# Attention of three transformer layers: banks dealt out anew in the forgetting attention, and ScalarE's copies ahead of its exponentials

## What is computed

```python
s = einsum('bqhd,bkhd->bhqk', qb, k) * scale
s = s + (cb[..., :, None] - c[..., None, :])      # c: running sum of log forget gates
s = where(qpos[:, None] >= kpos[None, :], s, -inf)
p = softmax(s, axis=-1)
out = einsum('bhqk,bkhd->bqhd', p, v)
```

## Time and profile before

| | busy us | share of the span |
|---|---|---|
| TensorE matmul | 2302.1 | 92% |
| VectorE | 1358.3 | 54% |
| ScalarE | 860.4 | 35% |
| GpSimd | 781.0 | 31% |

### The profile page before, as it was taken

The page is one execution under the profiler, slowest core; times in us unless marked ns, Lnnn a source line. Parts: engine busy times, 40 slices in busy tenths (PEclk is TensorE's granted clock), DMA queues, the critical chain, the costliest instruction groups (busy, mean ns, idle before and its releaser), DMA issues. The chain is left out here.

```text
span 2493.3 us, 32515 instructions
## 1 busy us (share of the span) xinstructions
PE 2302.1 (92%) x11689; PEld 1858.5 (75%) x11689; DVE 1358.3 (54%) x2272; ACT 860.4 (35%) x1347; POOL 781.0 (31%) x370
## 2 busy tenths in 40 slices
PE   5998998899999999898868899999998799999998
PEld 4777986778788888776756788877676557888876
DVE  4587655577604771465344577721497563677601
ACT  3425212433313332324323333322323564333322
POOL 2000001334443444332101444444464003344442
PEclk8999998999999999899887999999999899999999
DMA  3320001223332333232101333333332002233232
GB/s 116 93 77 1 1 2 32 72 81 100 98 96 78 99 101 101 73 93 58 45 18 35 93 93 100 97 86 87 89 85 60 1 1 85 84 93 93 87 98 85
DMA packets 346541, 179.78 MB, mean 72 GB/s; under 512 B 16840, under 2 KB 343619, under 8 KB 346443
## 3 DMA queue, kind: packets, MB, share of 16 engines
q1 hardware_dynamic: 344842, 177.36, 24.8%
q10 hardware_dynamic: 1056, 1.06, 0.1%
q0 software_dynamic: 544, 0.06, 0.0%
HBM read 176.33 MB, written 2.13 MB: 72 GB/s over the span
## 5 line engine op out<-in xcount | busy, mean ns | idle before, releaser
L298 POOL TENSOR_TENSOR wlo<-raw,whi 128x1024 fp32r<-128x1024 f32 (+3 forms) x327 | 743.0, 2276 | 1641.6 <-ACT whi L294 994.7
L311 PE MATMUL banks<-xhi,whi 128*128 128x512 f32 x1536 | 610.6, 398 | 5.1 <-DVE cb L1036 3.9
L313 PE MATMUL banks<-xhi,wlo 128*128 128x512 f32 x1536 | 601.6, 392 | 0.0
L312 PE MATMUL banks<-xlo,whi 128*128 128x512 f32 x1536 | 601.6, 392 | 0.0
L311 PEld LDWEIGHTS banks<-xhi,whi 128*128 128x128 f32 x1536 | 291.3, 190 | 72.8 <-issue 9.1
L312 PEld LDWEIGHTS banks<-xlo,whi 128*128 128x128 f32 x1536 | 291.2, 190 | 64.0 <-issue 3.8
L313 PEld LDWEIGHTS banks<-xhi,wlo 128*128 128x128 f32 x1536 | 290.6, 189 | 60.9
L877 ACT ACTIVATE whi<-raw 128x1024 fp32r<-128x1024 f32 (+1 forms) x216 | 209.8, 981 | 194.5 <-DMA raw<-in_ffn_w_out_dram 90.4
L965 ACT ACTIVATE cb<-banks,conv 128x512 f32<-128x512 f32 x152 | 118.0, 779 | 445.5 <-DVE banks L1025 445.5
L311 PE MATMUL banks<-ghi,whi 128*128 128x512 f32 x608 | 239.3, 394 | 19.8 <-DVE xT L1067 13.8
L312 PE MATMUL banks<-glo,whi 128*128 128x512 f32 x608 | 237.8, 391 | 0.0
(11 more groups left out here) (451 smaller groups left out, 3090.7 us busy)
## 6 DMA issues: line engine op xcount, KB each, us to landing
raw<-in_ffn_w_in_dram SPq DMA_DIRECT2D x88, 512.0 KB, 3.9
raw<-in_w_ffn_up_dram SPq DMA_DIRECT2D x64, 512.0 KB, 4.1
raw<-in_w_ffn_down_dram SPq DMA_DIRECT2D x32, 512.0 KB, 4.4
raw<-in_ev_w_in_dram SPq DMA_DIRECT2D x25, 512.0 KB, 4.0
raw<-in_ffn_w_out_dram SPq DMA_DIRECT2D x32, 384.0 KB, 3.7
raw<-in_ffn_w_out_dram SPq DMA_DIRECT2D x32, 320.0 KB, 3.3
raw<-in_od_w_in_dram SPq DMA_DIRECT2D x20, 512.0 KB, 3.9
raw<-in_w_in_dram SPq DMA_DIRECT2D x19, 512.0 KB, 3.9
```

What stands on the lines that cost most here:

```text
L298: return pool.tensor_tensor(wlo[c][:, 0:n, :], raw[b][:, 0:n, :], whi[c][:, 0:n, :].bitcast(F32), ALU.subtract)
L311: pe.matmul(acc, whi[b][:, k, :], hi(k), start=first and k == 0, stop=False)
L312: pe.matmul(acc, whi[b][:, k, :], lo(k), start=False, stop=False)
L313: mm = pe.matmul(acc, wlo[b][:, k, :], hi(k), start=False, stop=last and k == n - 1)
```

## The change

Stage C: score banks (0, 1) alone, turn banks 2 and 3, output banks 4 and 5, and banks 6 and 7 in turn for spreads and fillers. The sums move to step 1, the root to ScalarE's step 2, the spreads to steps 3 and 4 (two each), and the fillers to steps 7, 9, 11, 13, 15, 17, 18 and 19; a filler now waits for the add of the filler two before it. In every stage, ScalarE's step makes the copy of i-2 first and the exponentials of i second, and in stage B ScalarE copies the turned values ahead of the attention steps of its tile.

```diff
--- before.py
+++ after.py
@@ -1200,6 +1200,15 @@
             dve.tensor_copy(self.pt[n % 4][:, 0:w], bank[self.t_banks[n % len(self.t_banks)]][:, 0:w]).then_inc(self.ptaken[1].h, 1)
 
         def act(self, act, i):
+            u = i - self.FLIP
+            if 0 <= u < self.U:
+                w = self.units[u]["w"]
+                if u >= 2:
+                    act.wait_ge(self.weighed.h, u - 1)
+                act.wait_ge(self.flipped.h, u * self.J + 1)
+                to = 2 * w if self.joined else w
+                act.activation(self.pt[u * self.J % (2 * self.J)][:, 0:to], bank[self.t_banks[u * self.J % len(self.t_banks)]][:, 0:to], ACT.Copy)\
+                    .then_inc(self.ptaken[0].h, 1)
             u = i
             if u < self.U:
                 w, e = self.units[u]["w"], self.ex[u % self.NE]
@@ -1209,15 +1218,6 @@
                 if self.sink is not None:
                     ins = act.activation(self.f(u, "sink"), self.f(u, "sink"), ACT.Exp)
                 ins.then_inc(self.exped.h, 1)
-            u = i - self.FLIP
-            if 0 <= u < self.U:
-                w = self.units[u]["w"]
-                if u >= 2:
-                    act.wait_ge(self.weighed.h, u - 1)
-                act.wait_ge(self.flipped.h, u * self.J + 1)
-                to = 2 * w if self.joined else w
-                act.activation(self.pt[u * self.J % (2 * self.J)][:, 0:to], bank[self.t_banks[u * self.J % len(self.t_banks)]][:, 0:to], ACT.Copy)\
-                    .then_inc(self.ptaken[0].h, 1)
 
     def attend(units, sink=None, lam=None):
 
@@ -1997,6 +1997,10 @@
                     for t in (2 * (m - V0 - 5), 2 * (m - V0 - 5) + 1):
                         act.wait_ge(vb_turned.h, t + 1)
                         act.activation(vtb[:, t, :, :].rearrange("p m n -> p (m n)"), bank[4 + t % 2][:, :], ACT.Copy).then_inc(vb_taken.h, 1)
+                if A0 + 6 <= m < A0 + 10:
+                    t = m - A0 - 6
+                    act.wait_ge(va_turned.h, t + 1)
+                    act.activation(vta[:, t, :, :].rearrange("p m n -> p (m n)"), bank[7][:, :], ACT.Copy).then_inc(va_taken.h, 1)
                 for half in range(2):
                     if step(m, half) >= 0:
                         at.act(act, step(m, half))
@@ -2005,10 +2009,6 @@
                     chain(act.activation(y, af[0:NH, :], ACT.Abs))
                     chain(act.activation(y, y, ACT.Exp, scale=-1.0))
                     act.activation(y, y, ACT.Ln, bias=1.0).then_inc(did.h, 1)
-                if A0 + 6 <= m < A0 + 10:
-                    t = m - A0 - 6
-                    act.wait_ge(va_turned.h, t + 1)
-                    act.activation(vta[:, t, :, :].rearrange("p m n -> p (m n)"), bank[7][:, :], ACT.Copy).then_inc(va_taken.h, 1)
 
         @block.vector
         def _(dve):
@@ -2059,16 +2059,17 @@
                                       mask=(ident_r[:, :], mask_r[:, :]), bias=[forget[:, h, 0:w] for h in (2 * m, 2 * m + 1)],
                                       values=[[vta[:, b, m, p0:p0 + HD] for p0 in (0, HD)] for b in range(q + 1)],
                                       dst=oT[:, m, q * P:w]))
-            at = Attention(ctx, units, [(0, 1), (2, 3)], [4, 5], [6])
+            at = Attention(ctx, units, [(0, 1)], [2, 3], [4, 5])
             hi, lo = sb(ctx, "hi", [P, 4, S], F32R), sb(ctx, "lo", [P, 4, S], F32R)
             ob, sq, st, gain = oT[:, 4:8, :], sb(ctx, "sq", [P, 4, S]), sb(ctx, "st", [P, 3, 4 * NT]), sb(ctx, "gain", [P, 1])
             squared, summed, meaned, rooted, inverted, spread, finished, uppered, ready, half, added = (
                 sig(x) for x in ("squared", "summed", "meaned", "rooted", "inverted", "spread", "finished", "uppered", "ready", "half", "added"))
-            FIRST = 5
-
-            def part(i):
-
-                return (i - FIRST) // 2 if FIRST <= i < FIRST + 2 * n and (i - FIRST) % 2 == 0 else None
+            SUM, SPREAD = 1, 3
+            when = (7, 9, 11, 13, 15, 17, 18, 19)
+            part = {i: m for m, i in enumerate(when)}
+
+            def two(x):
+                return (2 * x, 2 * x + 1) if x in (0, 1) else ()
 
             def pool_part(pool):
                 for m in range(n):
@@ -2082,69 +2083,67 @@
 
             @block.tensor
             def _(pe):
-                for i in range(FIRST + 2 * n):
+                for i in range(at.U + 5):
                     at.pe(pe, i)
-                    if i == 0:
+                    if i == SUM:
                         for k in range(4):
                             pe.wait_ge(squared.h, k + 1)
                             for t in range(NT):
                                 mm = pe.matmul(bank[7][:, 4 * t + k:4 * t + k + 1], sq[:, k, t * P:(t + 1) * P], ones[:, 0:1], start=True, stop=True)
                         mm.then_inc(summed.h, 1)
-                    if 1 <= i < 5:
-                        k = i - 1
+                    for k in two(i - SPREAD):
                         pe.wait_ge(inverted.h, 1)
-                        if k:
-                            pe.wait_ge(finished.h, k + 1)
+                        if k >= 2:
+                            pe.wait_ge(finished.h, k)
                         for t in range(NT):
-                            mm = pe.matmul(bank[7][:, t * P:(t + 1) * P], st[:, 2, 4 * t + k:4 * t + k + 1].broadcast_to([P, P]), ident, start=True, stop=True)
+                            mm = pe.matmul(bank[6 + k % 2][:, t * P:(t + 1) * P], st[:, 2, 4 * t + k:4 * t + k + 1].broadcast_to([P, P]), ident, start=True, stop=True)
                         mm.then_inc(spread.h, 1)
-                    m = part(i)
-                    if m is not None:
+                    if i in part:
+                        m = part[i]
                         pe.wait_ge(w_lo.h, s0 + m + 1)
                         pe.wait_ge(ready.h, 4)
-                        if m:
-                            pe.wait_ge(added.h, m)
-                        three_passes(pe, bank[7][:, :], (s0 + m) % CUT, 4, lambda k: hi[:, k, :], lambda k: lo[:, k, :], True, True).then_inc(w_used.h, 1)
+                        if m >= 2:
+                            pe.wait_ge(added.h, m - 1)
+                        three_passes(pe, bank[6 + m % 2][:, :], (s0 + m) % CUT, 4, lambda k: hi[:, k, :], lambda k: lo[:, k, :], True, True).then_inc(w_used.h, 1)
 
             @block.scalar
             def _(act):
                 for k in range(4):
                     act.activation(sq[:, k, :], ob[:, k, :], ACT.Square).then_inc(squared.h, 1)
-                act.wait_ge(meaned.h, 1)
-                act.activation(st[:, 1, :], st[:, 0, :], ACT.Sqrt).then_inc(rooted.h, 1)
-                for i in range(FIRST + 2 * n):
+                for i in range(at.U + 5):
                     at.act(act, i)
-                    if 1 <= i < 5:
-                        k = i - 1
+                    if i == SUM + 1:
+                        act.wait_ge(meaned.h, 1)
+                        act.activation(st[:, 1, :], st[:, 0, :], ACT.Sqrt).then_inc(rooted.h, 1)
+                    for k in two(i - 1 - SPREAD):
                         act.wait_ge(finished.h, k + 2)
                         act.activation(hi[:, k, :], ob[:, k, :], ACT.Copy).then_inc(uppered.h, 1)
-                    m = part(i)
-                    if m is not None:
+                    if i in part:
+                        m = part[i]
                         split_hi(act, s0 + m + AHEAD)
 
             @block.vector
             def _(dve):
                 dve.tensor_scalar(gain[:, :], col("subln"), 1.0 - lam_init, None, ALU.mult).then_inc(finished.h, 1)
-                for i in range(FIRST + 2 * n):
+                for i in range(at.U + 5):
                     at.dve(dve, i)
-                    if i == 0:
+                    if i == SUM:
                         dve.wait_ge(summed.h, 1)
                         dve.tensor_scalar(st[:, 0, :], bank[7][:, 0:4 * NT], 1.0 / (2 * HD), EPS, ALU.mult, ALU.add).then_inc(meaned.h, 1)
+                    if i == SUM + 1:
                         dve.wait_ge(rooted.h, 1)
                         dve.reciprocal(st[:, 2, :], st[:, 1, :]).then_inc(inverted.h, 1)
-                    if 1 <= i < 5:
-                        k = i - 1
+                    for k in two(i - SPREAD):
                         dve.wait_ge(finished.h, 1)
                         dve.wait_ge(spread.h, k + 1)
-                        dve.scalar_tensor_tensor(ob[:, k, :], ob[:, k, :], gain[:, 0:1], bank[7][:, :], ALU.mult, ALU.mult).then_inc(finished.h, 1)
-                    if 2 <= i < 6:
-                        k = i - 2
+                        dve.scalar_tensor_tensor(ob[:, k, :], ob[:, k, :], gain[:, 0:1], bank[6 + k % 2][:, :], ALU.mult, ALU.mult).then_inc(finished.h, 1)
+                    for k in two(i - 2 - SPREAD):
                         dve.wait_ge(uppered.h, k + 1)
```

(6 more changed lines are left out.)

## The result

The changed kernel took 2439.77 us (median of 4 runs, 2429.89 to 2446.41), the kernel before 2506.53 beside it (4 runs, 2500.57 to 2513.09). The ratio is 0.973, interval 0.9686 to 0.9774: faster by 67 us. The forecast of 2443 holds. The profiled execution took 2438.76 us with a span of 2437.0, against 2495.1 and 2493.3.

What follows compares the result with a forecast made beforehand. TensorE, busy 92% of the span, was taken as the bound, losing time to waits and low clock. Gains of 40 (C), 17 (B), 3 (D) and 0 (A) sum to 60 us: 2502.7 - 60 = 2443, range 2432 to 2466.

Steps and rivals of the forecast that it cites:

- two output banks, the 27.1 us go: Stage C: with a second output bank the weighing needs an earlier store, so TensorE's 14 waits, 27.1 us, vanish.
- the tail: Stage C from step 16 on: last flips, weighings, fillers and add, put at 15.4 us.
- a mean clock above 0.9: Stage C: sign that the forecast is right, beside a length of 78 to 88 us.
- The start of C: Stage C, steps 0 to 7: 28.5 us of work, three waits of about 1 us, 2 us low clock; 33.5 together.
- The table loads: Stage C's start: still two loads, around the root; their price beyond the 1 us wait between 0 and 2.6 us.
- One score pair: Stage C: scores wait for the previous step's reduction, but other work covers it; cost nothing, upper bound 20 us.
- rival 2: Stage C: the one score pair becomes the bound, TensorE waiting 1.3 us each step; 2463 us, chance 0.08.
- Stage B, forecast 17: Stage B: 10.2 us of waits go, 2 from copies ahead of exponentials, 5 from the clock; 17 us gained.
- Stage D, forecast 3: Stage D: flips wait for the scaling instead of ScalarE's copy, 0.6 us won in five places; 3 us with clock.
- rival 1: Stage C: the clock stays at 0.76 though the waits go, so C gains only 25; 2464 us, chance 0.11.
- rival 3: Stage B: the change fails there or leaves a wait of like size from something else late; 2460 us, chance 0.05.
- rival 4: Stage C: TensorE and VectorE alternate strictly at low clock, 5.6 us a step; slower, 2517 us, chance 0.03.

Runs made afterwards that it cites:

- banks only: Only stage C's banks and step plan changed against the kernel before, ScalarE keeping exponentials before copies and turned values behind the attention steps: ratio 0.9835.

## Why the prediction was right, point by point

- **Stage C, forecast 122.3 to 82: 122.6 to 81.6.** The step "two output banks, the 27.1 us go" holds, by the one-output-bank kernel as well as by the waits. Steps 8 to 15 were put at 32 us and took 31.5, at a clock of 1.00 (windows below, second row); the tail was put at 15.4 and took 15.0 (third row), with its one wait of 1.1 us before the flips of unit 15 as forecast. The sign "a mean clock above 0.9" was met only just, 0.90 here and 0.88 in three later profiles of the same plan; in this profile all of the low clock lies at the stage's start.

```profile
1220.50:1255.50 35.00, 33.13 (x210) 26.66 (x210) 21.04 (x74) 18.87 (x50) 0.00 (x0) 0.76 0.00 1
1255.50:1287.00 31.50, 31.25 (x234) 23.30 (x234) 20.39 (x76) 15.25 (x45) 5.27 (x5) 1.00 0.12 34
1287.00:1302.00 15.00, 12.91 (x87) 9.92 (x85) 5.76 (x13) 2.87 (x5) 4.96 (x4) 1.00 0.24 71
1240.50:1302.00 61.50, 58.59 (x438) 44.29 (x436) 39.63 (x132) 26.73 (x74) 10.23 (x8) 1.00 0.12 35
```

- **The start of C, forecast 33.5 and 1 for rests of low clock: 35.0 (first row).** The total is near by two errors that cancel. The waits were put at 3 us; 35.0 less 33.1 busy leaves 1.9. The clock was put at 3 us (2 and 1); 0.76 over 35.0 us is 16.8 us at the lower level, half of which, 8.4 us, the low clock costs. Two spreads show it:

```profile
1222.84 6.16 PE L2092 MATMUL banks<-cst,sq 128*128 128x1 f32 x32
...
1236.45 3.78 PE L2099 MATMUL banks<-cst,st 128*128 128x128 f32 x16
...
1242.48 2.05 PE L2099 MATMUL banks<-cst,st 128*128 128x128 f32 x16
```

  The first pair took 3.78 us at the low clock, the second 2.05, against 2.12 in the sum. So the steps were priced too high, by nearly 4 us (35.0 less 1.9 and 8.4 leaves 24.7 for the 28.5), the waits by 1, and the clock was put some 5 too low. The near total is luck.
- **The table loads.** Put at 1 us inside the startup waits, bounds 0 and 2.6. The root and the reciprocal behind it cost VectorE 1.98 us of idle time, and TensorE waits in none of it for the spreads:

```profile
1233.63 1.28 ACT L2117 ACT_TABLE_LOAD   x1
1234.92 0.22 ACT L2117 ACTIVATE st<-st 128x16 f32<-128x16 f32 x1
1235.17 0.25 DVE L2135 RECIPROCAL st<-st 128x16 f32<-128x16 f32 x1 [1.98 <-ACT st L2117]
```

  The Trainium skill, "ScalarE: Activation LUTs", section "What ACT_TABLE_LOAD costs", counts 2.66 us for each switch, the load of 1.28 and a drain of 1.38. This trace has the 1.28, but no room for the drain: ScalarE's instruction before the load ends at 1233.61, the root starts 0.01 us after the load, and from the load's start to the reciprocal that needs the root are 1.54 us.
- **One score pair.** "Cost nothing, with hardly 0.1 us of cover at 384" holds from step 8 on: at the step in question the weight load waits 0.17 us for the reduction and the scores themselves don't wait. Before that scores do wait for a reduction, the sign that was named for rival 2: three waits of 0.5 to 0.7, 1.8 us in all, in steps 1, 3 and 7, of which only the first was forecast. In the kernel with two pairs they are gone.
- **Stage B, forecast 17, bounds 11 and 19: 19.2,** just past the upper bound. All 10.2 us of waits went and the copies' order gave 2.9 for 2. The clock, put at 5 and at most 6.6, gave about 6: 107.8 us at 0.94 hold 13 us at the low level. The term of the clock was a little small.
- **Stage D, forecast 3, bounds 0 and 6: 5.9.** The mechanism is as forecast, with the flips waiting for the scaling instead of ScalarE's copy. But the forecast read one row of waits where the kernel before has two in front of the flips, and took 0.6 us off in five places:

```profile
PE banks L1133 <- ACT pt L1219: 8.2, 8, 2.0
PE banks L1133 <- DVE ex L1181: 2.0, 3, 0.9
```

  These 11 waits of 10.2 us became 9 of 8.4, so 1.8 us of waits went and not 3. Idle time by the windows went from 10.9 to 9.3, which is 1.6; the other 4 us are busy time, 41.7 to 37.6, from a clock of 0.93 instead of 0.84. The order is real (50.5 to 53.8 us in the three profiles with the old one, 44.9 to 46.9 in the nine with the new), and most of its size lies in the clock, a term that the forecast had only named: this is the mis-sized one. What moved D's clock is not shown; it read 0.90 for 0.84 with nothing in D changed (banks only).
- **Stage A, forecast 0: 0.8,** with 37.5 to 39.2 us over all kernels without ScalarE's store: no difference that can be told.
- **The rivals.** Clock (rival 1): C has its 17 low microseconds at the start and reads 1.00 from 1240.5 to the end (fourth row of the windows above). The rule of the Trainium skill that was set against the change ("TensorE: Matmul & The Clock Gate", section "A second HAM failure mode: psum-queue depth-cycling") isn't borne out here: all eight banks are cycled through for 61.5 us with only short idle pieces, 58.6 us of it busy, and the clock stays up. The page's own case is bf16 with 512 columns, which no run here repeats. One pair as the bound (rival 2): no, 1.8 us instead of 20. Another wait in B (rival 3): none left. Strict alternation (rival 4): a step of 8 to 15 takes 3.9 us with its half of a filler in it (31.5 / 8), below the 4.7 from which it would decide.
- **Profile and median.** The forecast put the profiled execution at 2435 and the median 7.6 above it, as before; they were 2438.8 and 2439.8. The offset was no property of the kernel, only of which execution had been profiled. That both came within 4 us is partly luck: the stages gave 7 us more than forecast, and the untouched stretch took 9.6 back in the profile.
- **Not in the forecast** was the wander of the untouched 900 us, 21 us between the extremes of single profiles. The sum of the stages was 66.9 for a forecast of 60; the span fell by 56.3 and the medians by 66.8.

## What to carry to other kernels

When an engine makes an operation last in its step and another waits for it one step later, one more buffer can be worth the whole wait and the clock that goes with it: here one PSUM bank gave about 42 us, while the waits that a second score pair could have ended came to 1.8. Before moving banks, price each by the wait that it ends, and look in the timeline for what is last in each engine's step. A copy on which the bound engine waits belongs ahead of work that has cover, and a wait can be worth more than its length: in B 10.2 us of waits, three of up to 4.1, brought 16.3. An engine's busy time does not say whether it sets the pace: in D taking over 3 us of work from VectorE made nothing shorter, while opening the ring of dependences gave 4.

## What the runs showed that was not expected

- 32 matmuls of one column took 6.16 us, all but the first microsecond at the low clock, and 8 of four columns 1.02. With the short ones TensorE was back at full clock some 7 us sooner, 5.1 of them the sums' own time.
- The same instructions of one stage run at different clocks from one profile to the next: D with the new order took 44.9 us at 1.00 (two score pairs in C) and 46.9 at 0.93 (the changed kernel), and the recurrent layer's stretch 904.5 to 925.5. What is won by a stage of 5 us is seen in the stage and not in the total.
- VectorE's reciprocal of 128x16 took 0.25 us (the row above, 1235.17), and one of 128x512 took 3353 ns, elsewhere in the same kernel. Its line among the groups (busy us, mean ns of one, idle before it):

```profile
L2298 DVE RECIPROCAL part<-sq 128x512 f32<-128x512 f32 x1 | 3.4, 3353 | 0.0
```
